# The order of sixteen attention units: four and four, or by turns

## The reference, cut to what matters

```
o1 = attend(dq[:, :, :, 0, None, :], dk[:, :, :, 0, :], dv)      # 4 differential heads
o2 = attend(dq[:, :, :, 1, None, :], dk[:, :, :, 1, :], dv)
od = (o1 - lam * o2)                                             # value width 128
od = rmsnorm(od, subln_g) * (1.0 - lambda_init)
og = attend(gq.reshape(B, S, 2, 4, 64), gk, gv)                  # 8 grouped heads, 2 key heads
o = concatenate([od, og]) @ w_out
```

## Time and profile before

| what | value |
|---|---|
| median of 3 runs | 1583.6 us (1581.93 to 1584.01) |
| the profiled execution, own time | 1578.86 us |
| its span in the profile | 1577.1 us |
| PE busy | 1351.5 us (86%) |
| DVE busy | 1087.2 us (69%) |
| ACT busy | 604.3 us (38%) |
| POOL busy | 277.0 us (18%) |
| chain that ended last | PE 50%, DMA 17%, DVE 15%, issue 10%, POOL 5%, ACT 3% |
| first attention, 134 to 197 us (63 us) | PE busy 49.7 us, DVE 50.86 us, ACT 36.98 us |

### The profile page before, as it was taken

The page is one execution under the profiler, slowest core; times in us unless marked ns, Lnnn a source line. Parts: engine busy times, 40 slices in busy tenths (PEclk is TensorE's granted clock), DMA queues, the critical chain, the costliest instruction groups (busy, mean ns, idle before and its releaser), DMA issues.

```text
span 1577.1 us, 19834 instructions
## 1 busy us (share of the span) xinstructions
PE 1351.5 (86%) x6224; PEld 939.6 (60%) x6224; DVE 1087.2 (69%) x2252; ACT 604.3 (38%) x1227; POOL 277.0 (18%) x263
## 2 busy tenths in 40 slices
PE   7998879769797979798887787879999978799998
PEld 2775675424243434343443336669998766699986
DVE  4698745676767667676777656867886467678863
ACT  5244641122222222213132125455665344666652
POOL 0000000634444444444434400000000000000000
PEclk9999979989898989889898888999999989999999
DMA  9525320999999999999999993423545424244540
GB/s 398 203 107 213 125 111 27 377 421 421 422 422 422 422 422 421 421 422 422 422 422 421 421 386 126 160 108 114 208 161 187 162 82 160 108 160 162 193 154 27
DMA packets 49264, 415.76 MB, mean 264 GB/s; under 512 B 5408, under 2 KB 5536, under 8 KB 6560
## 3 DMA queue, kind: packets, MB, share of 16 engines
q0 software_dynamic: 36864, 268.45, 40.9%
q1 hardware_dynamic: 12320, 146.29, 24.5%
HBM read 413.67 MB, written 1.05 MB: 263 GB/s over the span
## 4 chain that ended last, share of the span: by engine, by line
PE 50%; DMA 17%; DVE 15%; issue 10%; POOL 5%; ACT 3%; DVEq 0%; POOLq 0%; ACTq 0%; SPq 0%
DMA arena<-in_uv,ids 15%; PE ps L990 8%; PE ps L1235 5%; PE ps L1234 5%; PE ps L1236 5%; PE ps L1061 4%; PE ps L1063 4%; PE ps L1062 4%; POOL arena L724 3%; POOL ring L724 2%; DVE ring L1853 2%; DMA ring<-in_b1w 2%; PE ps L1053 2%; PE ps L843 1%; PE ps L845 1%
## 5 line engine op out<-in xcount | busy, mean ns | idle before, releaser
L990 PE MATMUL ps<-ring,arena 128*128 128x512 f32 x512 | 255.2, 662 | 107.4 <-ACT arena L1408 107.4
L990 PEld LDWEIGHTS ps<-ring,arena 128*128 128x128 f32 x512 | 107.8, 214 | 250.3 <-issue 130.9
L1853 DVE CUSTOM_DVE_ANT_0 arena<-arena 128x1024 f32<-128x1024 f32 x128 | 156.7, 1225 | 134.6 <-DMA arena<-in_uv,ids 134.5
L724 POOL DMA_INDIRECT ring<-in_uv,ids x128 | 145.0, 1133 | 536.8 <-issue 308.3
L990 PE MATMUL ps<-arena 128*128 128x512 f32 x512 | 226.3, 598 | 9.3 <-ACT arena L1408 9.2
L558 DVE TENSOR_TENSOR arena_r<-ring,arena_r 128x1024 fp32r<-128x1024 f32 x152 | 185.2, 1224 | 66.4 <-ACT arena_r L543 66.3
L1234 PE MATMUL ps<-hH,arena_r 128*128 128x256 f32 x704 | 199.4, 283 | 0.0
L1235 PE MATMUL ps<-arena_r 128*128 128x256 f32 x704 | 199.3, 283 | 0.0
L1236 PE MATMUL ps<-hH,arena_r 128*128 128x256 f32 x704 | 199.3, 283 | 0.0
L543 ACT ACTIVATE arena_r<-ring 128x1024 fp32r<-128x1024 f32 x152 | 159.0, 1053 | 64.8 <-PE ps L1063 64.8
L990 PEld LDWEIGHTS ps<-arena 128*128 128x128 f32 x512 | 96.8, 191 | 137.2 <-issue 115.6
(11 more groups left out here) (283 smaller groups left out, 2054.6 us busy)
## 6 DMA issues: line engine op xcount, KB each, us to landing
ring<-in_lw SPq DMA_DIRECT2D x40, 2048.0 KB, 7.6
ring<-in_b1w SPq DMA_DIRECT2D x18, 2048.0 KB, 9.0
wqb<-in_wq SPq DMA_DIRECT2D x8, 1024.0 KB
ring<-in_lw SPq DMA_DIRECT2D x6, 1024.0 KB, 5.2
ring<-in_lw SPq DMA_DIRECT2D x2, 1088.0 KB, 10.8
ring<-in_uv,ids POOLq DMA_INDIRECT x128, 22.6
arena<-in_uv,ids POOLq DMA_INDIRECT x128, 25.9
cst<-in_const SPq DMA_DIRECT2D x1, 1483.5 KB, 20.4
```

What stands on the lines that cost most here:

```text
L724: pool.indirect_dma_start(pairs_at[k], None, uv, bass.IndirectOffsetOnAxis(ap=ids[:, c, k:k + 1], axis=0))\
L990: last = nc.tensor.matmul(ps[:, 4 + 2 * c + b, :], diag[:, k % 4, :], vrows[k][:, b * 512:(b + 1) * 512], start=False, stop=(close and k = ...
L1853: V.tensor_tensor_reduce(out=urows[k], in0=urows[k], in1=hrow[:, c, :], scale=1.0, scalar=0.0, op0=ALU.mult, op1=ALU.add, accum_out=dots[: ...
```

## The change

`units()` lists the eight tiles of a token block in another order. Differential and grouped tiles come by turns: 0, 4, 1, 5, 2, 6, 3, 7. Since the engines all walk this list, each engine's list of instructions changes alike; buffers, waits, counts and the pieces of `mod_part` tied to the number m stay as they are.

```diff
@@ -589,7 +589,7 @@
         def units():
-            return [(c, t) for c in range(NC) for t in range(8)]
+            return [(c, t) for c in range(NC) for t in (0, 4, 1, 5, 2, 6, 3, 7)]
 
         def act_pt(act, m):
```

## The result

The changed kernel takes 1571.4 us (median of 13 runs, 1567.07 to 1578.98) and the kernel before 1581.74 us (13 runs, 1576.05 to 1584.29). The ratio is 0.9942, 95% interval 0.993 to 0.9955: 9.2 us faster, between 7.1 and 11.1 (the two medians alone differ by 10.3 us). The forecast was 6.0 us. The side was right, and so was what it says of the loops; PE's clock at the end of the attention was not.

A forecast was written before the change was run, and what follows sets the result against it. It took two loops to bound the attention by turns, DVE's and that of PE and ACT. Alternating gains 4.9 us up to unit 15's transposes and 1.26 behind, taken as 6: 1583.6 - 6.0 = 1577.6 us, range 1573 to 1583.5.

The forecast's parts named there:

- the loops: First attention: differential units loop through DVE in 4.15 us, grouped units through PE and ACT in 4.48 us.
- What bounds: First attention, 134 to 210 us: DVE bounds four differential units, PE and ACT the next four grouped; 8.0 us a pair.
- The ring: Longest way round a differential and grouped pair, through DVE and PE: 7.66 us, or 7.4 with the short L455.
- the closing edge: DVE's maximum L1717 of odd units waits for PE's scores, some 0.4 us.
- The 0.86 us of lower clock at the start: Units 2 to 4: PE's lower clock slows the values of unit 0 again, adding 0.86 us to the 7.66.
- Transposes of unit 15: PE, end of the attention: they start at 195.1 to 195.5 us instead of 200.28, 4.9 us gained.
- Behind unit 15: Last values on PE: the first are differential, 1.84 us for 3.10 at the lower clock, 1.26 us less.
- The same fall at the end: PE's clock drops to the lower level behind the last units as before, after about 3.0 us of work in 190 to 196.
- The raised clock: Rival: PE's clock stays up at the attention's end, some 3.4 us less, -9 us in all, 1574.6 us; chance 0.2.
- the pairs don't overlap: Rival: each pair of units pays for both loops, 8.63 us, sum about 0, 1583.6 us; chance 0.17.
- PE's clock falls within the loop: Rival: PE runs at the lower level between pairs, 7 us slower with all six, 1590.6 us; chance 0.07.
- Behind the attention: Output projection, norm and experts: the 6 us pass on one for one; rival that they are lost there, chance 0.06.

The follow-up runs named there:

- max_behind: Changed kernel with DVE's two mod_part pieces put ahead of the maximum of unit m+2; ratio 0.9941 to the kernel before, attention 65.70 us.
- before_again: The kernel before, unchanged, profiled a second time; attention 76.65 us, against 76.74 us in its first profile.
- before_filler: The kernel before plus 15 unused PE matmuls, placed where PE idles at units 0, 1, 14 and 15; ratio 0.9967 to the kernel before.
- grouped_first: The kernel before with tiles by turns, grouped unit first in each pair (4, 0, 5, 1, 6, 2, 7, 3); ratio 0.9992 to the kernel before.
- max_behind_filler: Changed kernel with DVE's mod_part pieces ahead of the maximum, plus 15 unused PE matmuls; ratio 0.9935 to the kernel before.

## Why the prediction was wrong, and where it was right

- **What bounds.** Right. Two loops with different bounds, and one ring through both where they alternate.
- **The ring.** Right, to 0.02 us: 7.66 and 7.4 forecast, 7.66 and 7.39 measured. The wait of L609 for L891 fell to 7.1 us (below 8 forecast), and DVE's busy time is the same to 1 us. DVE's wait at the closing edge was put at 0.4 us and is 0.37 to 0.45. Counted from the first scores the reciprocals of units 2, 8 and 14 were to be at 11.3, 34.9 and 56.8, and stand at 11.4, 34.1 and 56.1.
- **The 0.86 us of lower clock at the start.** Wrong twice. It came in both profiles of before, but cost 0.4 us there (the reciprocal of unit 3 at 16.8 us, and at 16.4 with filler). And in neither profile of the changed kernel did it come.
- **Transposes of unit 15.** 4.9 us earlier by the sum; 5.6 against the profile of before (66.70 to 61.07), and 5.3 at equal clock (66.32 to 61.06). The sum had charged the 0.86 us that did not come.
- **Behind unit 15.** 1.26 us by the sum, at the lower clock; 1.0 at the full one (6.95 to 5.96). That both add up to the same 6.2 us is in part luck: the first term was 0.3 too small and the second 0.3 too large.
- **The same fall at the end.** This is the step that failed, and with it the 6.0 us. I wrote that the stretch ahead "holds about 3.0 us of work, no denser, so I expect the same fall". Measured, it was denser: in the 6 us that end with the transposes of unit 15 PE is busy 3.29 us in the changed kernel and 2.80 in before; in the ten it is 7.16 and 6.19. And the same fall did not come: of the five profiles with the new end four held the full level, and the fifth was back after 4 us. Behind unit 15 the time went from 10.0 us to 7.2 and 6.0, that is by 2.9 and 4.1 us and not by 1.26. The lower level there cost the old order 3.1 us (10.04 for 6.95). The raised clock stood among the rivals at -9 us, and the measured -9.2 is that rival. It had put 3.4 us on the new order's tail, which no profile shows at the lower level throughout; the 3.1 are the old order's. Its chance of 0.2 was too low. What decides the level beside PE's idle time stays open.
- **The other rivals.** That the pairs don't overlap, and that PE's clock falls within the loop, are both out: PEclk is 1.00 from 138 to 196 in the changed kernel. What the Trainium skill says of cycling through PSUM banks ("TensorE: Matmul & The Clock Gate", A second HAM failure mode: psum-queue depth-cycling) didn't show within the loop.
- **Behind the attention.** Nothing was given back: from the table load to the end both profiles agree to 1.2 us, the changed kernel being the shorter.

The range failed for another reason. Its lower end already held the raised clock, but it was laid from a median of three runs, 1583.6, that 13 runs put at 1581.7. Laid from that, its lower end is 1571.1, and the measured 1571.4 is inside.

## What to carry to other kernels

Where a loop has two kinds of steps with different bounds and buffers for only two steps, it can pay to put the kinds by turns: find the longest ring through both by walking the waits; its edges can be read off the old trace. Which kind comes first matters, since extra work tied to a step number then lands inside the ring or beside it. And price the end of a stage apart at both clock levels: the lower level behind the last loops cost half as much here (3.1 us) as the whole reordering gained (6.2).

## What the runs showed of the hardware

I had not expected PE's clock to explain so much of the scatter between executions. In the 31 runs of the kernel before that were taken beside max_behind, the mean granted clock and the time go together (correlation -0.81; -0.73 and -0.65 in the two other sets, of 24 and 23), which is about half of the scatter or more. From the first key matmul to the first L1234 the profiles fall into two groups: 815.3 to 816.6 us in nine, 812.8 to 813.3 in five. Old, new and mixed orders are in both groups, and before and before_again, the same instructions, are one in each. Three of the four profiles with unused matmuls are in the shorter group and two of the ten without; whether the matmuls have a part in that is not shown. I read one profile of each group. The stretch in which the last group of experts begins, in before and then in before_filler (columns as in the earlier trace rows):

```profile
928.50:933.50 5.00, 5.00 (x8) 2.15 (x9) 2.60 (x5) 1.32 (x5) 0.00 (x0) 0.67 0.71 297
```

```profile
925.90:930.90 5.00, 3.42 (x8) 1.63 (x9) 2.64 (x6) 1.48 (x5) 0.00 (x0) 1.00 0.92 382
```

The chains of the two show the cost, before and then before_filler, whose lines stand 7 further down (L997 is L990):

```profile
928.40 15.71 PE ps L990 x32
...
956.62 6.66 PE ps L1053 x32
```

```profile
927.48 14.02 PE ps L997 x32
...
954.02 5.21 PE ps L1060 x32
```

It is 1.7 us in the last products and 1.45 in the first matmuls of the next stage. A kernel's ratio holds this scatter too, so the orders are compared above by the attention's own time.

What stays open: which idle time decides the level. The share of busy time doesn't settle it alone. grouped_first kept the full level behind 5.97 busy us of ten, and max_behind_filler lost it behind 9.00.
